# A chunked recurrence's gate: where its constants are finished, who takes an absolute value, and where a logarithm is added

## The chip, the cores and the metric

One core of one Trainium2 chip runs the whole kernel. The metric is the device time in microseconds (us) from the start to the end of one execution. The kernel before took 1930.76 us, the median of 3 runs (1929.14 to 1933.79). TensorE (PE in the profile) multiplies, VectorE (DVE), ScalarE (ACT) and GpSimd (POOL) work on elements, SyncE issues the weight loads.

## The reference

256 tokens of width 1024 pass through one block with gated linear attention and local attention, then through two layers of another kind. Each of these two layers normalizes x, projects it, computes latent attention and a recurrence (`_hgrn2`), and adds the joined result times `w_out` to x; a dense feed-forward part follows in layer 0, eight experts in layer 1. What matters here is the gate of the recurrence:

```python
lb_p = jax.nn.softmax(hg_lower_bounds, axis=0)        # two rows, 512 columns
lower = jnp.cumsum(lb_p, axis=0) - lb_p[0:1]          # layer 0: 0; layer 1: the second row's share
f = lb + (1.0 - lb) * jax.nn.sigmoid(z)
log_f = jnp.log(jnp.maximum(f, F_FLOOR))
k = (1.0 - lb) * jax.nn.sigmoid(-z)
...
b = jnp.cumsum(log_f)                                 # inside a chunk
attn = einsum(q, k, exp(b_t - b_s));  state += (k * exp(b_last - b_s))^T v
```

The lower bound is 0 in layer 0, so there log f and log k need nothing but z. In layer 1 log k = log(1 - lb) + log sigmoid(-z). The kernel computes keys as logarithms: `n_k` holds -log k, and `soft` = ln(1 + exp(-|z|)) serves both log sigmoids.

## The kernel before

All products with large weights run on TensorE in three passes: each weight piece ("sub", 128 x 1024 words) is split into a rounded part `w_hi` (ScalarE, line 1379, in `split_to`) and the rest `w_lo`, which GpSimd makes outside of the feed-forward parts (line 632) and VectorE inside of them. There are four buffers for each, and a piece is 12 matmuls of 512 columns (lines 696 to 698). ScalarE's program interleaves these splits with its own work by hand: `split_to(n)` issues all splits up to piece n, and each of them waits until TensorE has used the piece four before it.

Each engine runs one list of instructions in order, and semaphores join them. TensorE's list for a layer l is: the projections `hf_l` (four pieces, the gate's z), `hq_l` (four), `hg_l` (four), `c0_l`, `c1_l`, `hi_l`, then small products, then the output projection `wo_l` (eight pieces). Between the second and third piece of `hg_l` stands `turn_gate`: the running sums of log f (`hb`, 16 matmuls, line 1026), the turned keys (`hkT`, 8 transposes, line 781) and the tail sums (`ht`, line 1031). Its outputs go to four PSUM banks used in turn, so `ht`, the fifth, waits until VectorE has copied the first `hb` bank out (line 1752). After the fourth piece of `hg_l` the queries are turned (line 781 again), and `level(0)` (line 1049) after the first piece of `c0_l` waits until VectorE has copied them.

The gate on the other engines, in the kernel before:

- VectorE scales z out of PSUM (line 2123), takes |z| (line 2126, recorded at 1768), waits for ScalarE's ln(1 + exp(-|z|)) (lines 1549 and 1551).
- Layer 0: it makes `n_lf` (line 2130) and `n_k` (line 2131), and then finishes the bounds, which only layer 1 reads: a sum (2133), a reciprocal over 512 columns (2134), a product over 1024 (2135, recorded at 1756), and a small constant (2136).
- Layer 1: it forms f in four steps (2140 to 2144), ScalarE takes ln f (1557), VectorE makes `n_lf` (2147) and subtracts log(1 - lb), `log_rest`, from `n_k` over 128 x 1024 (2149).
- Then in both layers the two `hb` banks are copied to `n_bT` (1752), ScalarE makes exp of the turned keys (1562, one instruction of 512 columns a bank), VectorE adds them to `n_bT` (2155, one of 512 a bank), forms the tail keys `n_kt` (2158) and goes on to `level_diff(1)` (two instructions at 2174) and the copies of the turned queries (1752).

Layer 0's output projection `wo_0` takes its input from two splits on VectorE, `split_out("mixT_0", ...)`, the second after the recurrence's output gate. Then VectorE waits for the first half of `wo_0` and adds it to x in `residual` (line 2047). TensorE turns that new x (line 770, `turn_x` in `out_gemm`) before the last piece of `wo_0`.

Of the kernel before, what the change touches and what calls it, by code (L numbers as in the profile page):

```python
# [28 lines left out]
ALU = mybir.AluOpType  # L29
# [157 lines left out]
def build(nc, A, out):  # L187
# [80 lines left out]
    with ExitStack() as ctx:  # L268
        sems = {}

        def sem(name):
            if name not in sems:
                sems[name] = ctx.enter_context(nc.semaphore(name))
            return sems[name]
# [67 lines left out]
        def tiles(ap, t=T):  # L342
            return ap.rearrange("p (t n) -> p t n", t=t)
# [31 lines left out]
        c_gain = [tiny(5) for _ in range(2)]  # L375
        ss, ms, root, rinv, rinv_q = tiny(2 * T), tiny(T), tiny(T), tiny(T), tiny(T)
        least_rest = tiny(1)
        head_ms, head_rinv = tiny(20), tiny(20)
        row_max, sink_exp, row_sum, row_rec = tiny(16), tiny(16), tiny(16), tiny(16)
        sinks = tiny(SWA_HEADS)  # L380
# [922 lines left out]
        def _(act):  # L1303
# [236 lines left out]
            for l in range(2):  # L1540
                squares(range(2 * T), [(f"x_ffn_{l}", q + 1) for q in range(2 * T)], f"ss_l{l}")
                factor(f"l{l}")
                if l == 0:
                    split_to(span["hf_0"][1] + 2)
                    act.wait_ge(sem("bounds_shifted"), 1)
                    act.activation(bounds, bounds, ACT.Exp).then_inc(sem("bounds_exp"), 1)
                split_to(span[f"hf_{l}"][1] + BUFFERS + 1)
                act.wait_ge(sem("z_abs"), l + 1)
                act.activation(n_tmp[0], n_tmp[0], ACT.Exp, scale=-1.0).then_inc(sem("z_odds"), 1)
                act.wait_ge(sem("z_odds"), l + 1)  # L1550
                act.activation(n_tmp[1], n_tmp[0], ACT.Ln, bias=1.0).then_inc(sem("z_soft"), 1)
                if l == 1:
                    act.activation(log_rest, bound_rest, ACT.Ln, bias=least_rest).then_inc(sem("rest_log"), 1)
                split_to(span[f"hg_{l}"][0] + 2)
                if l == 1:
                    act.wait_ge(sem("f_ready"), 1)
# [2 lines left out]
                for t in range(T):  # L1559
                    j = pair_at[f"hkT_{l}"] + t  # L1560
                    act.wait_ge(sem("pair_full"), j + 1)
                    act.activation(n_kT[:, t * 512:(t + 1) * 512], pair_bank[j % 4][:, :], ACT.Exp, scale=-1.0) \
                        .then_inc(sem("k_turned"), 1)
                evacuate(f"hq_{l}", by_token(n_q, 0, func=ACT.Silu))
                evacuate(f"hg_{l}", by_token(n_g, 0, func=ACT.Silu))

# [169 lines left out]
        def _(dve):  # L1736
            told = counter()

            def link(instruction):

                instruction.then_inc(sem("vector_step"), 1)
                dve.wait_ge(sem("vector_step"), told("vector_step"))
# [370 lines left out]
            for l in range(2):  # L2113
# [9 lines left out]
                    dve.tensor_scalar(n_z[:, t, :], gemm_bank[(gemm_at[f"hf_{l}"] + t) % 4][:, :], rinv[:, t:t + 1],  # L2123
                                      LEAST_LOGIT, ALU.mult, ALU.max).then_inc(sem("gemm_read"), 1)
                dve.wait_ge(sem("gemm_read"), gemm_at[f"hf_{l}"] + T)
                absolute(tiles(n_tmp[0]), n_z, "z_abs")
                soft = tiles(n_tmp[1])
                if l == 0:
                    dve.wait_ge(sem("z_soft"), 1)
                    dve.scalar_tensor_tensor(n_lf, n_z, 0.0, soft, ALU.min, ALU.subtract).then_inc(sem("n_lf_ready_0"), 1)  # L2130
                    dve.scalar_tensor_tensor(n_k, n_z, 0.0, soft, ALU.max, ALU.add).then_inc(sem("n_k_ready"), 1)
                    dve.wait_ge(sem("bounds_exp"), 1)
                    link(dve.tensor_tensor(bound_sum, bound_rest, bound_low, ALU.add))
                    link(dve.reciprocal(bound_sum, bound_sum))
                    mul(bounds, bounds, over(bound_sum, 1, 2))
                    link(dve.tensor_scalar(least_rest, ident[:, 0:1], 0.0, LEAST_REST, ALU.mult, ALU.add))
                else:
                    odds, share = tiles(n_tmp[0]), tiles(n_tmp[2])
                    dve.wait_ge(sem("z_odds"), 2)
                    link(dve.scalar_tensor_tensor(share, n_z, 0.0, odds, ALU.is_ge, ALU.max))  # L2140
                    mul(share, share, over(bound_rest, 1, T))
                    dve.wait_ge(sem("z_soft"), 2)
                    link(dve.scalar_tensor_tensor(odds, odds, 1.0, over(bound_low, 1, T), ALU.add, ALU.mult))
                    dve.tensor_tensor(odds, odds, share, ALU.add).then_inc(sem("f_ready"), 1)
                    link(dve.scalar_tensor_tensor(n_k, n_z, 0.0, soft, ALU.max, ALU.add))
                    dve.wait_ge(sem("f_log"), 1)
                    dve.tensor_tensor(n_lf, odds, soft, ALU.subtract).then_inc(sem("n_lf_ready_1"), 1)
                    dve.wait_ge(sem("rest_log"), 1)
                    dve.tensor_tensor(n_k, n_k, over(log_rest, 1, T), ALU.subtract).then_inc(sem("n_k_ready"), 1)
                for t in range(T):  # L2150
                    copy_out(f"hb_{l}", t, n_bT[:, t * 512:(t + 1) * 512])
                for t in range(T):
                    part = slice(t * 512, (t + 1) * 512)
                    dve.wait_ge(sem("k_turned"), T * l + t + 1)
                    dve.tensor_tensor(n_kb[:, part], n_bT[:, part], bank_of(f"hkT_{l}", t)[:, :], ALU.add) \
                        .then_inc(sem("pair_read"), 1)
                    dve.wait_ge(sem("pair_read"), told("pair_read"))
                dve.tensor_tensor(n_kt, bank_of(f"ht_{l}", 0)[:, :], n_k[:, 0, :], ALU.subtract).then_inc(sem("pair_read"), 1)
                dve.wait_ge(sem("pair_read"), told("pair_read"))

                def blocks(a, half):
# [126 lines left out]
                split_out(f"mixT_{l}", banks=range(0, 2), freed=span[f"hi_{l}"][1])  # L2288
                gate_hgrn()
                split_out(f"mixT_{l}", banks=range(2, 4))  # L2290
                residual(f"_{l}", f"x_mixed_{l}", f"g{l}")
                if l == 0:
                    norm("g0")
# [198 lines left out]
```

## Time and profile before

| what | us |
|---|---|
| median of 3 runs | 1930.76 (1929.14 to 1933.79) |
| the profiled execution, whole | 1933.04 |
| its span, first to last instruction | 1931.1 |
| TensorE busy | 1892.8 |
| VectorE busy | 1501.8 |
| ScalarE busy | 1244.5 |
| GpSimd busy | 392.2 |

The span is what the profile covers; 1.9 us of the execution lie around it. Busy time of an engine says how full its list is; what matters for a change is the idle time of TensorE, and what ended each piece of it. Layer 0's gate stands at about 480 to 505 us of the span, its output projection at 588 to 614, layer 1's gate at 813 to 845; the experts begin after 960.

### The profile page before, as it was taken

How to read it: one execution, taken by the hardware profiler on the slowest of the kernel's cores; microseconds unless marked ns; L12 is line 12 of the kernel's file. 1: busy time of each engine (PE TensorE's matmuls, PEld its weight loads, DVE VectorE, ACT ScalarE, POOL GpSimd, SP SyncE). 2: the span in 40 equal slices, each digit the busy share in tenths (PEclk: the TensorE clock that was granted, in tenths of full speed). 3: DMA queues.
4: the chain of work that ended last, by engine and by line, in shares of the span. 5: the costliest groups of instructions: out<-in, count | busy, mean ns of one | idle time of the engine just before them, and what ended most of it. 6: DMA issues, size and time to landing. Idle time of an engine off the chain costs nothing.

```text
span 1931.1 us, 27217 instructions
## 1 busy us (share of the span) xinstructions
PE 1892.8 (98%) x9931; PEld 1610.5 (83%) x9931; DVE 1501.8 (78%) x1598; ACT 1244.5 (64%) x1473; POOL 392.2 (20%) x204
## 2 busy tenths in 40 slices
PE   8999999999999999999899999999999999999997
PEld 6788889998888999878788888888888888888885
DVE  7755366666765756697599999999999999899997
ACT  5654444445644444564388887888888888888885
POOL 5856870002823000372430000000000000000000
PEclk9999999999999999999899999999999999999999
DMA  9434556664443766434399999999999999999994
GB/s 279 154 130 131 175 185 214 216 225 153 140 125 122 226 214 215 156 119 141 131 377 394 382 395 357 395 396 355 395 354 396 396 353 395 355 395 395 358 395 175
DMA packets 251402, 524.54 MB, mean 272 GB/s; under 512 B 10009, under 2 KB 58785, under 8 KB 251185
## 3 DMA queue, kind: packets, MB, share of 16 engines
q1 hardware_dynamic: 244000, 506.36, 73.5%
q10 hardware_dynamic: 5088, 10.03, 1.4%
q0 software_dynamic: 2224, 6.96, 1.1%
q8 instruction: 55, 0.90, 0.2%
q14 instruction: 35, 0.28, 0.0%
HBM read 508.12 MB, written 15.20 MB: 271 GB/s over the span
## 4 chain that ended last, share of the span: by engine, by line
PE 90%; DVE 6%; issue 2%; ACT 2%; POOL 1%; DMA 0%; DVEq 0%; SPq 0%; ACTq 0%
PE bank L696 27%; PE bank L698 27%; PE bank L697 27%; PE bank L1049 2%; PE bank L1222 1%; DVE w_lo_sb L1797 1%; PE bank L770 1%; PE bank L743 1%; PE bank L749 1%; POOL w_lo_sb L632 1%; ACT w_hi_sb L1359 0%; PE bank L1102 0%; PE bank L1100 0%; PE bank L904 0%; PE bank L881 0%
## 5 line engine op out<-in xcount | busy, mean ns | idle before, releaser
L1797 DVE TENSOR_TENSOR w_lo_sb<-arena,w_hi_sb 128x1024 fp32r<-128x1024 f32 x672 | 806.8, 1223 | 73.8 <-ACT w_hi_sb L1359 47.6
L1359 ACT ACTIVATE w_hi_sb<-arena 128x1024 fp32r<-128x1024 f32 x672 | 710.5, 1062 | 165.1 <-PE bank L698 164.6
L696 PE MATMUL bank<-w_hi_sb,left_hi_sb 128*128 128x512 f32 (+1 forms) x1424 | 563.9, 396 | 7.5 <-POOL w_lo_sb L632 3.0
L698 PE MATMUL bank<-w_hi_sb,left_lo_sb 128*128 128x512 f32 (+1 forms) x1424 | 552.7, 388 | 0.0
L697 PE MATMUL bank<-w_lo_sb,left_hi_sb 128*128 128x512 f32 (+1 forms) x1424 | 552.1, 388 | 0.0
L1379 ACT ACTIVATE w_hi_sb<-arena 128x1024 fp32r<-128x1024 f32 (+1 forms) x269 | 280.3, 1052 | 336.6 <-PE bank L698 325.2
L632 POOL TENSOR_TENSOR w_lo_sb<-arena,w_hi_sb 128x1024 fp32r<-128x1024 f32 (+1 forms) x134 | 343.0, 2580 | 566.2 <-ACT w_hi_sb L1379 565.7
L696 PEld LDWEIGHTS bank<-w_hi_sb,left_hi_sb 128*128 128x128 f32 x1424 | 268.4, 188 | 66.4 <-issue 6.3
L698 PEld LDWEIGHTS bank<-w_hi_sb,left_lo_sb 128*128 128x128 f32 x1424 | 268.2, 188 | 56.1
L697 PEld LDWEIGHTS bank<-w_lo_sb,left_hi_sb 128*128 128x128 f32 x1424 | 268.5, 189 | 52.2 <-issue 0.7
L1809 DVE TENSOR_TENSOR w_lo_sb<-arena,w_hi_sb 128x1024 fp32r<-128x1024 f32 x135 | 163.8, 1219 | 126.1 <-ACT w_hi_sb L1379 125.1
L696 PE MATMUL bank<-w_hi_sb,hid_hi_sb 128*128 128x512 f32 x656 | 257.3, 392 | 0.0
L697 PE MATMUL bank<-w_lo_sb,hid_hi_sb 128*128 128x512 f32 x656 | 255.5, 389 | 0.0
L698 PE MATMUL bank<-w_hi_sb,hid_lo_sb 128*128 128x512 f32 x656 | 255.4, 389 | 0.0
L696 PE MATMUL bank<-left_hi_sb,w_hi_sb 128*128 128x256 f32 (+1 forms) x712 | 201.7, 283 | 0.1
L698 PE MATMUL bank<-left_hi_sb,w_lo_sb 128*128 128x256 f32 (+1 forms) x712 | 201.4, 283 | 0.0
L697 PE MATMUL bank<-left_lo_sb,w_hi_sb 128*128 128x256 f32 (+1 forms) x712 | 201.4, 283 | 0.0
L687 POOL DMA_INDIRECT h_sb<-returned,arena x2 | 2.6, 1278 | 841.9 <-DMA returned<-arena 841.6
L698 PEld LDWEIGHTS bank<-w_hi_sb,hid_lo_sb 128*128 128x128 f32 x656 | 123.1, 188 | 26.0
L696 PEld LDWEIGHTS bank<-w_hi_sb,hid_hi_sb 128*128 128x128 f32 x656 | 123.3, 188 | 24.4
L697 PEld LDWEIGHTS bank<-w_lo_sb,hid_hi_sb 128*128 128x128 f32 x656 | 123.4, 188 | 24.2
L696 PEld LDWEIGHTS bank<-left_hi_sb,w_hi_sb 128*128 128x128 f32 (+1 forms) x712 | 135.9, 191 | 1.2 <-DVE w_lo_sb L1809 0.3
(328 smaller groups left out, 1628.3 us busy)
## 6 DMA issues: line engine op xcount, KB each, us to landing
arena<-in_moe_w_gate SPq DMA_DIRECT2D x112, 1024.0 KB, 7.8
arena<-in_moe_w_up SPq DMA_DIRECT2D x112, 1024.0 KB, 7.8
arena<-in_moe_w_down SPq DMA_DIRECT2D x112, 1024.0 KB, 7.6
arena<-in_w_in SPq DMA_DIRECT2D x45, 1024.0 KB, 5.1
arena<-in_w_ffn_in SPq DMA_DIRECT2D x22, 1024.0 KB, 6.2
arena<-in_w_out SPq DMA_DIRECT2D x12, 1024.0 KB, 5.0
arena<-in_w_ffn_out SPq DMA_DIRECT2D x11, 1024.0 KB, 4.8
arena<-in_dense_w_gate SPq DMA_DIRECT2D x11, 1024.0 KB, 5.9
```

Of the source, the lines that this page charges most:

```text
L632: pool.tensor_tensor(buffer(w_lo_sb, j, k, n), w, buffer(w_hi_sb, j, k, n).bitcast(F32), ALU.subtract).then_inc(sem("w_lo_by_gpsimd"), 1)
L696: pe.matmul(out, still[0], moving[0], start=start, stop=False)
L697: pe.matmul(out, still[0], moving[1], start=False, stop=False)
L698: return pe.matmul(out, still[1], moving[0], start=False, stop=stop)
L743: pe.matmul(gemm_bank[turned % 4][:, j * TOKENS:(j + 1) * TOKENS], w[:, k, j, 0:NOPE], n_cT[:, first + k, :], start=(k == 0), stop=(k == k ...
L749: mm = pe.matmul(o, n_cT[:, first + k, t * P:(t + 1) * P], w[:, k, :, NOPE:], start=(k == 0), stop=(k == k_tiles - 1))
L770: tr = pe.transpose(b[:, at:at + P], source(k, t), ident)
L1049: mm = pe.matmul(b[:, i * P:(i + 1) * P], key[:, at:at + P], query[:, at:at + P], start=True, stop=True)
L1359: act.activation(expert_buffer(w_hi_sb, j), expert_piece(j % MOE_SUBS), ACT.Copy) \
L1379: act.activation(buffer(w_hi_sb, j, *w.shape[1:]), w, ACT.Copy).then_inc(sem("w_hi_ready"), 1)
L1797: dve.tensor_tensor(expert_buffer(w_lo_sb, j), expert_piece(j % MOE_SUBS), expert_buffer(w_hi_sb, j).bitcast(F32), ALU.subtract) \
L1809: dve.tensor_tensor(buffer(w_lo_sb, j, *w.shape[1:]), w, buffer(w_hi_sb, j, *w.shape[1:]).bitcast(F32), ALU.subtract) \
```

## The change

- In layer 0 the bounds are no longer finished after `n_k`, but after the second `mixT_0` split and ahead of `residual`. Two instructions join them there: the product of `bound_rest` with the identity (128 x 512) and its sum over the last axis, which turns 1 - lb so that it lies along partitions, one column for each of the four heads (`rest_turned`).
- |z| is taken by ScalarE with `Abs` in both layers, ahead of the exponential. The one split that stood ahead of the exponential now stands behind it.
- In layer 1 `n_k` is no longer reduced by `log_rest`. ScalarE takes one more small logarithm (`rest_turned`, 128 x 4), and its exp of the turned keys becomes four instructions of 128 columns a bank with a bias column each. VectorE's add to `n_bT` becomes four `scalar_tensor_tensor` of 128 columns a bank, and `n_kt` gets `log_rest` in a second instruction (128 x 512).

```diff
-                split_to(span[f"hf_{l}"][1] + BUFFERS + 1)
+                split_to(span[f"hf_{l}"][1] + BUFFERS)
+                act.wait_ge(sem("gemm_read"), gemm_at[f"hf_{l}"] + T)
+                act.activation(tiles(n_tmp[0]), n_z, ACT.Abs).then_inc(sem("z_abs"), 1)
                 act.wait_ge(sem("z_abs"), l + 1)
                 act.activation(n_tmp[0], n_tmp[0], ACT.Exp, scale=-1.0).then_inc(sem("z_odds"), 1)
                 act.wait_ge(sem("z_odds"), l + 1)
+                split_to(span[f"hf_{l}"][1] + BUFFERS + 1)
                 act.activation(n_tmp[1], n_tmp[0], ACT.Ln, bias=1.0).then_inc(sem("z_soft"), 1)
                 if l == 1:
                     act.activation(log_rest, bound_rest, ACT.Ln, bias=least_rest).then_inc(sem("rest_log"), 1)
+                    act.activation(rest_turned, rest_turned, ACT.Ln, bias=least_rest).then_inc(sem("rest_log"), 1)
...
-                    act.activation(n_kT[:, t * 512:(t + 1) * 512], pair_bank[j % 4][:, :], ACT.Exp, scale=-1.0) \
-                        .then_inc(sem("k_turned"), 1)
+                    # layer 0 as before; layer 1:
+                    for i in range(HG_HEADS):
+                        ins = act.activation(n_kT[:, t * 512 + i * P:t * 512 + (i + 1) * P],
+                                             pair_bank[j % 4][:, i * P:(i + 1) * P], ACT.Exp,
+                                             bias=rest_turned[:, i:i + 1], scale=-1.0)
+                    ins.then_inc(sem("k_turned"), 1)
...
-                absolute(tiles(n_tmp[0]), n_z, "z_abs")
...
-                    dve.wait_ge(sem("bounds_exp"), 1)
-                    link(dve.tensor_tensor(bound_sum, bound_rest, bound_low, ALU.add))
-                    link(dve.reciprocal(bound_sum, bound_sum))
-                    mul(bounds, bounds, over(bound_sum, 1, 2))
-                    link(dve.tensor_scalar(least_rest, ident[:, 0:1], 0.0, LEAST_REST, ALU.mult, ALU.add))
...
-                    dve.wait_ge(sem("rest_log"), 1)
-                    dve.tensor_tensor(n_k, n_k, over(log_rest, 1, T), ALU.subtract).then_inc(sem("n_k_ready"), 1)
...
+                        dve.wait_ge(sem("rest_log"), 2)
+                        for i in range(HG_HEADS):
+                            at = slice(t * 512 + i * P, t * 512 + (i + 1) * P)
+                            ins = dve.scalar_tensor_tensor(n_kb[:, at], turned[:, i * P:(i + 1) * P],
+                                                           rest_turned[:, i:i + 1], n_bT[:, at], ALU.subtract, ALU.add)
...
+                    link(dve.tensor_tensor(n_kt, bank_of(f"ht_{l}", 0)[:, :], n_k[:, 0, :], ALU.subtract))
+                    dve.tensor_tensor(n_kt, n_kt, log_rest, ALU.add).then_inc(sem("pair_read"), 1)
...
                 split_out(f"mixT_{l}", banks=range(2, 4))
+                if l == 0:
+                    dve.wait_ge(sem("bounds_exp"), 1)
+                    link(dve.tensor_tensor(bound_sum, bound_rest, bound_low, ALU.add))
+                    link(dve.reciprocal(bound_sum, bound_sum))
+                    mul(bounds, bounds, over(bound_sum, 1, 2))
+                    link(dve.tensor_scalar(least_rest, ident[:, 0:1], 0.0, LEAST_REST, ALU.mult, ALU.add))
+                    picked = n_tmp[2][:, 0:512].rearrange("p (g d) -> p g d", d=P)
+                    mul(picked, bound_rest.rearrange("p (g d) -> p g d", d=P), over(ident, 1, HG_HEADS))
+                    link(dve.tensor_reduce(rest_turned, picked, AX_X, ALU.add))
                 residual(f"_{l}", f"x_mixed_{l}", f"g{l}")
```

## Rows read from the trace of the kernel before

**Rows 1.** The page, engines: busy us, share of the span, instructions.
```profile
PE 1892.8 (98%) x9931; PEld 1610.5 (83%) x9931; DVE 1501.8 (78%) x1598; ACT 1244.5 (64%) x1473; POOL 392.2 (20%) x204
```
**Rows 2.** TensorE's waits, 476 to 620 us: total us, times, longest.
```profile
PE bank L1031 <- DVE arena L1752: 1.4, 1, 1.4
PE bank L696 <- POOL w_lo_sb L632: 0.7, 2, 0.4
```
**Rows 3.** TensorE's waits, 800 to 935 us.
```profile
PE bank L1026 <- DVE arena L2147: 1.8, 1, 1.8
PE bank L781 <- DVE arena L2149: 1.3, 1, 1.3
PE bank L696 <- POOL w_lo_sb L632: 0.3, 1, 0.3
```
**Rows 4.** VectorE in order of time, layer 0's gate: start us, us, what.
```profile
481.36 2.32 DVE L1768 SCALAR_TENSOR_TENSOR arena<-arena 128x1024 f32<-128x1024 f32 x1
...
489.32 3.42 DVE L2131 SCALAR_TENSOR_TENSOR arena<-arena 128x1024 f32<-128x1024 f32 x1
492.67 2.88 DVE L2133 TENSOR_TENSOR arena<-const_sb 128x512 f32<-128x512 f32 x1
495.58 3.35 DVE L2134 RECIPROCAL arena<-arena 128x512 f32<-128x512 f32 x1
498.96 2.25 DVE L1756 TENSOR_TENSOR const_sb<-const_sb,arena 128x1024 f32<-128x1024 f32 x1
```
**Rows 5.** GpSimd in order of time, layer 0's gate.
```profile
482.55 3.40 POOL L632 TENSOR_TENSOR w_lo_sb<-arena,w_hi_sb 128x1024 fp32r<-128x1024 f32 x1
```
**Rows 6.** ScalarE in order of time, layer 0's gate (idle before, its releaser).
```profile
483.41 1.06 ACT L1379 ACTIVATE w_hi_sb<-arena 128x1024 fp32r<-128x1024 f32 x1 [1.09 <-PE bank L698]
```
**Rows 7.** VectorE in order of time, layer 0's output projection.
```profile
605.56 1.28 DVE L2047 TENSOR_TENSOR x_sb<-x_sb,bank 128x512 f32<-128x512 f32 x2 [5.76 <-PE bank L698]
```
**Rows 8.** GpSimd in order of time, the same stretch.
```profile
597.63 2.40 POOL L632 TENSOR_TENSOR w_lo_sb<-arena,w_hi_sb 128x1024 fp32r<-128x1024 f32 x1 [0.39 <-ACT w_hi_sb L1379]
...
603.97 2.40 POOL L632 TENSOR_TENSOR w_lo_sb<-arena,w_hi_sb 128x1024 fp32r<-128x1024 f32 x1 [0.38 <-ACT w_hi_sb L1379]
606.63 2.39 POOL L632 TENSOR_TENSOR w_lo_sb<-arena,w_hi_sb 128x1024 fp32r<-128x1024 f32 x1 [0.26 <-ACT w_hi_sb L1379]
```
**Rows 9.** TensorE in order of time, turning the new x.
```profile
608.02 1.03 PE L770 MATMUL bank<-const_sb,x_sb 128*128 128x128 f32 x8
```
**Rows 10.** VectorE in order of time, layer 1's gate.
```profile
828.53 1.23 DVE L2144 TENSOR_TENSOR arena<-arena 128x1024 f32<-128x1024 f32 x1
...
839.09 4.35 DVE L2174 TENSOR_TENSOR arena<-arena 128x512 f32<-128x512 f32 x2
843.45 1.42 DVE L1752 COPY arena<-bank 128x512 f32<-128x512 f32 x2
```
**Rows 11.** ScalarE in order of time, layer 1's gate.
```profile
829.79 1.06 ACT L1557 ACTIVATE arena<-arena 128x1024 f32<-128x1024 f32 x1 [6.16 <-DVE arena L2144]
830.76 3.88 ACT L1379 ACTIVATE w_hi_sb<-arena 128x1024 fp32r<-128x1024 f32 x4
834.65 1.28 ACT L1562 ACT_TABLE_LOAD   x1
```
**Rows 12.** TensorE in order of time, layer 1.
```profile
835.54 1.09 PE L781 MATMUL bank<-const_sb,arena 128*128 128x128 f32 x8 [1.26 <-DVE arena L2149]
...
846.41 1.95 PE L1049 MATMUL bank<-arena 128*128 128x128 f32 x16
```
**Rows 13.** Groups by line and shape: count, busy us, mean ns.
```profile
L1786 DVE SCALAR_TENSOR_TENSOR left_lo_sb<-bank,small_sb,left_hi_sb 128x256 fp32r<-128x256 f32 x48 | 21.0, 480 | 0.8
L1455 ACT ACTIVATE h_sb<-h_sb,small_sb 128x128 f32<-128x128 f32 x8 | 3.1, 390 | 4.9 <-DVE small_sb L1764 4.9
```
**Rows 14.** Busy time in two stretches: PE, PEld, DVE, ACT, POOL, granted clock, DMA share, GB/s.
```profile
813.00:846.00 33.00, 29.67 (x143) 23.82 (x143) 30.59 (x20) 22.18 (x24) 28.54 (x11) 1.00 0.43 135
...
952.00:962.50 10.50, 7.37 (x36) 6.63 (x34) 6.75 (x26) 4.01 (x8) 2.72 (x4) 0.51 0.17 52
```

More of the change, by code:

```diff
@@ L377, in build @@
         least_rest = tiny(1)
+        rest_turned = tiny(HG_HEADS)
         head_ms, head_rinv = tiny(20), tiny(20)
@@ L1561, in _ @@
                     act.wait_ge(sem("pair_full"), j + 1)
-                    act.activation(n_kT[:, t * 512:(t + 1) * 512], pair_bank[j % 4][:, :], ACT.Exp, scale=-1.0) \
-                        .then_inc(sem("k_turned"), 1)
+                    if l == 0:
+                        act.activation(n_kT[:, t * 512:(t + 1) * 512], pair_bank[j % 4][:, :], ACT.Exp, scale=-1.0) \
+                            .then_inc(sem("k_turned"), 1)
+                        continue
+                    if t == 0:
+                        act.wait_ge(sem("rest_log"), 2)
+                    for i in range(HG_HEADS):
[3 more added lines that the diff above has]
+                    ins.then_inc(sem("k_turned"), 1)
                 evacuate(f"hq_{l}", by_token(n_q, 0, func=ACT.Silu))
@@ L2144, in _ @@
                     dve.tensor_tensor(odds, odds, share, ALU.add).then_inc(sem("f_ready"), 1)
-                    link(dve.scalar_tensor_tensor(n_k, n_z, 0.0, soft, ALU.max, ALU.add))
+                    dve.scalar_tensor_tensor(n_k, n_z, 0.0, soft, ALU.max, ALU.add).then_inc(sem("n_k_ready"), 1)
                     dve.wait_ge(sem("f_log"), 1)
                     dve.tensor_tensor(n_lf, odds, soft, ALU.subtract).then_inc(sem("n_lf_ready_1"), 1)
-                    dve.wait_ge(sem("rest_log"), 1)
-                    dve.tensor_tensor(n_k, n_k, over(log_rest, 1, T), ALU.subtract).then_inc(sem("n_k_ready"), 1)
                 for t in range(T):
@@ L2154, in _ @@
                     dve.wait_ge(sem("k_turned"), T * l + t + 1)
-                    dve.tensor_tensor(n_kb[:, part], n_bT[:, part], bank_of(f"hkT_{l}", t)[:, :], ALU.add) \
+                    turned = bank_of(f"hkT_{l}", t)
+                    if l == 0:
+                        dve.tensor_tensor(n_kb[:, part], n_bT[:, part], turned[:, :], ALU.add) \
+                            .then_inc(sem("pair_read"), 1)
+                    else:
+                        dve.wait_ge(sem("rest_log"), 2)
[3 more added lines that the diff above has]
+                                                           rest_turned[:, i:i + 1], n_bT[:, at], ALU.subtract, ALU.add)
+                        ins.then_inc(sem("pair_read"), 1)
+                    dve.wait_ge(sem("pair_read"), told("pair_read"))
+                if l == 0:
+                    dve.tensor_tensor(n_kt, bank_of(f"ht_{l}", 0)[:, :], n_k[:, 0, :], ALU.subtract) \
                         .then_inc(sem("pair_read"), 1)
-                    dve.wait_ge(sem("pair_read"), told("pair_read"))
-                dve.tensor_tensor(n_kt, bank_of(f"ht_{l}", 0)[:, :], n_k[:, 0, :], ALU.subtract).then_inc(sem("pair_read"), 1)
+                else:
+                    link(dve.tensor_tensor(n_kt, bank_of(f"ht_{l}", 0)[:, :], n_k[:, 0, :], ALU.subtract))
+                    dve.tensor_tensor(n_kt, n_kt, log_rest, ALU.add).then_inc(sem("pair_read"), 1)
                 dve.wait_ge(sem("pair_read"), told("pair_read"))
@@ L2290, in _ @@
                 split_out(f"mixT_{l}", banks=range(2, 4))
+                if l == 0:
+                    dve.wait_ge(sem("bounds_exp"), 1)
[6 more added lines that the diff above has]
+                    link(dve.tensor_reduce(rest_turned, picked, AX_X, ALU.add))
                 residual(f"_{l}", f"x_mixed_{l}", f"g{l}")
```

## The prediction

> **What bounds the kernel now.** I read the page first, then TensorE's waits around the two gates, then the instructions in order of time on each engine there. On the page TensorE is busy for 1892.8 of 1931.1 us [rows 1]: the kernel ends with TensorE, and an edit elsewhere is worth only the TensorE idle time that it ends or makes. The waits name that idle time. Layer 0's gate has 1.4 us before the tail sums (the first `hb` bank was not copied out, because VectorE was still finishing the bounds) and 0.7 us in two waits for GpSimd's `w_lo` [rows 2]. Layer 1's gate has 1.8 us for `n_lf`, 1.3 us for `n_k` and 0.3 us for GpSimd [rows 3].
>
> The order of time shows a second thing, on which most of this prediction rests. A `w_lo` piece takes GpSimd 2.40 us [rows 8], but 3.40 us while VectorE works on two SBUF operands [rows 5]. Four VectorE instructions of the gate are long as well: the 512-wide sum takes 2.88 us and the 1024-wide ones 2.25 to 3.42 us [rows 4], where a free 1024-wide one takes 1.23 us [rows 10] and a 512-wide one reading PSUM takes about 0.7 us (two in 1.42 us, [rows 10]). The two engines take turns: each such VectorE instruction lets a running GpSimd piece finish, and the next piece waits for it. Instructions on PSUM keep their length beside GpSimd. The Trainium skill (SBUF — State Buffer, section "Who interferes with whom") says the same as a rule: a VectorE instruction with two SBUF inputs and a GpSimd one that reads SBUF exclude each other for their whole length, and whichever issues first wins; the trace agrees (2.88 us against about 0.7).
>
> **Layer 0's gate: minus 2.5 us.** The bounds leave: 8.5 us of VectorE from 492.67 on, so that the `hb` bank is copied as soon as it is full, and the 1.4 us wait goes. |z| leaves VectorE (2.32 us, [rows 4]); it stood between two GpSimd pieces and cost the second 1.0 us (3.40 against 2.40, [rows 5, 8]). With |z|, the sum and the product gone, GpSimd's pieces come 1 to 2 us sooner, which ends one wait of 0.3 us of the two in [rows 2] (the other, 0.4 us, stands at 480.29, ahead of the change) and some slow restarts, by my estimate another 0.5 to 0.8 us. What ScalarE gains, `Abs`, is hidden: its 1.06 us (taken from the 1024-wide logarithm, [rows 11]) fall into the 1.09 us in which ScalarE waited for TensorE to free a buffer [rows 6], and that split now runs behind the exponential; the logarithm starts at the same time. `n_lf` may lose 1.4 us to a GpSimd piece, still 5 us ahead of its reader. Without the GpSimd part the gain is 1.4 us; with every stall gone it is 2.8 us. I take 2.5.
>
> No row shows an `Abs`. If it made ScalarE load its table again, that would cost 1.28 us as at [rows 11], once in each layer, between nothing and 1.3 us on `n_lf`, of which layer 0 hides all and layer 1 part. The Trainium skill (ScalarE: Activation LUTs, "Table sets: the hidden batching unit") says that `abs` lies in every set, hence no load; the sum is the same by it.
>
> **Layer 0's output projection: plus 3.4 us.** VectorE is free from 599.80, and `residual` starts at 605.56 after 5.76 us of idle time [rows 7]. TensorE wants the new x at 608.02 [rows 9]; `residual`'s two adds end at 606.84, so it may come 1.2 us late at no cost. Into this gap go: sum 0.7 + reciprocal 3.35 [rows 4] + product 1.2 + constant 0.15 + product with the identity 0.7 + reduction 0.7 + five links of 0.03, together 6.95 us. With no other engine in the way they end at 606.75, `residual` at 608.05: a cost of about 0.1 us, the lower bound. But both products have two SBUF operands, and GpSimd works through this stretch [rows 8]. The sum waits until the piece of 597.63 ends at 600.0 [rows 8] and ends at 600.6; the reciprocal (one operand; 3.35 us beside GpSimd already) ends at 603.98; the big product issues at about 604.02, GpSimd's piece at 603.97.
> - If GpSimd wins: product from 606.4 to 607.5, next piece (issued at 606.63) to 609.9, product with the identity to 610.5, reduction to 611.2. `residual` starts 5.7 us late; minus 1.2 of slack, TensorE waits 4.5 us.
> - If VectorE wins: product to 605.2, piece to 607.6, identity product to 608.2, reduction to 608.9: 3.4 late, TensorE waits 2.2 us.
>
> The order hangs on 0.05 us, which I can't call; I take the middle, 3.4, and keep 0.1 and 4.5 as bounds. Everything behind `residual` (the split of the turned x, the squares, ScalarE's splits) moves with it; GpSimd is a piece or two ahead of TensorE there and absorbs its own delay.
>
> **Layer 1's gate: plus 1.1 us.** First the gain. |z| on ScalarE saves up to 1.3 us before the exponential, but the f chain then falls between GpSimd's pieces again: followed piece by piece, f is ready at about 829.1 instead of 829.76 [rows 10]. So `n_lf` ends 0.7 us sooner and the first `hb` matmul starts at 831.55 instead of 832.24. `n_k` is ready before it, its subtraction gone: the 1.3 us wait before the transposes goes [rows 3]. TensorE leaves `turn_gate` 2.1 to 2.2 us sooner and would be at `level(0)` at 844.3 instead of 846.41 [rows 12].
>
> But `level(0)` needs the turned queries, which VectorE copies behind `level_diff(1)`; before, those copies end at 844.87 [rows 10], 1.5 us ahead. Their new time: ScalarE runs ln f and the four splits 0.7 us sooner, loads its table and starts the exponentials at 835.25 [rows 11]. They are now eight of 390 ns [rows 13]; back to back I take 0.3 us each, 2.4 us together (1.09 before), so they end at 837.7. VectorE's eight 128-wide adds, read down from 480 ns at 256 columns [rows 13], take 1.2 us a bank and follow ScalarE: 838.9 instead of 838.33. The tail keys take 0.7 us, to 839.6; their second instruction has two SBUF operands and waits for GpSimd, which has a backlog of four pieces from 831.5 on (to 840.95): it ends at 841.55. So `level_diff(1)` starts 2.4 us later than 839.09. Its two instructions take turns with GpSimd:
> - If GpSimd's next piece (issued at about 841.3) is ahead of the first, they end at 847.5, the copies at 848.95: `level(0)` at 849.0, plus 2.6 us.
> - If it comes after, they end at 845.1, the copies at 846.5: plus 0.1 us.
> - If the second tail instruction finds GpSimd free: copies at 845.9, minus 0.4 us.
> - Were VectorE not the later one at all, the whole 2.2 us would stay.
>
> I take plus 1.1, between the first two. Later readers in the layer have 2.7 us or more to spare.
>
> **Sum.** -2.5 + 3.4 + 1.1 = +2.0 us. The profiled execution took 1933.04, 2.3 above the median of the runs; against the median the forecast is 1932.8 us.
>
> **The rivals.**
> - *The moved work is covered and both gates keep their gain.* Layer 0 gains 2.5 and loses 0.1, layer 1 gains 0.4 to 2.2: 2.8 to 4.6 us faster, about 1927. For it: VectorE did idle 5.76 us where the bounds go. Against it: that idle time is shorter than the work even without GpSimd, and GpSimd is busy for more than two thirds of it. Chance 0.22.
> - *VectorE becomes the bound in both places, each time because a GpSimd piece gets in ahead.* Place: before `turn_x` in `wo_0` and before `level(0)` in layer 1. Price: 4.5 + 2.6 - 2.5 = +4.6 us, 1935.4. It decides by whether the products issue after 603.97 and the first difference after about 841.3. Chance 0.20.
> - *The longer wait drops TensorE's clock.* After the router's waits the granted clock is 0.51 for 10.5 us [rows 14], that is 1.2 GHz, with TensorE busy 7.37 us. A 4.5 us wait at 608 might do the same and cost up to 5 us more: 1938 to 1940. Against it, TensorE was idle for 3.3 of 33 us around layer 1's gate and the clock stayed at 1.00, that is 2.4 GHz [rows 14]. Chance 0.05.
> - *The forecast*, gains and new waits that nearly cancel, 1930.3 to 1934.5: 0.53.
>
> A measurement of this kernel tells a change from none at about 0.2%, 3.9 us. Of the first rival three fifths lie beyond it (0.14 faster, and 0.02 for what I overlooked); of the second most and the third all (0.22). The rest, 0.62, is within. The range 1927.0 to 1936.5 reaches to both sides.
>
> **What would show each step.** Right: no wait of line 1031 for 1752 in layer 0; GpSimd's pieces near 2.4 us from 482 on; no wait for `n_k` in layer 1; a new wait of TensorE at `turn_x` (line 770 family) for `residual` of 2 to 4.5 us, with the two products of the bounds longer than 1.2 and 0.7 us; a new wait at `level(0)` for the query copies. The prediction is wrong if the product with the identity takes 0.7 us and `turn_x` doesn't wait, or if `level_diff(1)` starts before 840.

## The result: 0.5% slower, outside the predicted range

| | before | after |
|---|---|---|
| median, us | 1929.26 (1929.11 to 1933.79, 5 runs) | 1939.96 (1938.98 to 1940.96, 5 runs) |
| ratio | 1 | 1.0050, 95% interval 1.0039 to 1.0061 |
| profiled execution, us | 1933.04 | 1938.98 |
| its span, us | 1931.1 | 1937.1 |
| granted clock, mean | 0.996 | 0.991 |

The forecast was 1932.8 us, in a range of 1927.0 to 1936.5. The change costs about 10 us, and 2.0 were expected. First the page of the kernel after, engines as in [rows 1], and the granted clock in 40 slices:

```profile
PE 1895.5 (98%) x9931; PEld 1613.5 (83%) x9931; DVE 1489.4 (77%) x1604; ACT 1247.9 (64%) x1482; POOL 385.7 (20%) x204
...
PEclk9999999999998999999899999999999999999999
```

VectorE works 12.4 us less, and TensorE has as many instructions as before but is busy 2.7 us longer. So something other than waiting has been added: the same matmuls took longer. Next TensorE's waits from 476 to 620 us, which answer to [rows 2] (us in total, times, longest):

```profile
PE bank L771 <- DVE x_sb L2061: 4.1, 1, 4.1
...
PE bank L697 <- POOL w_lo_sb L633: 0.4, 1, 0.4
```

and from 800 to 935 us, which answer to [rows 3]:

```profile
PE bank L1050 <- DVE arena L1766: 3.8, 1, 3.8
...
PE bank L1027 <- DVE arena L2155: 1.4, 1, 1.4
```

The waits for `hb` in layer 0 and for `n_k` in layer 1 are gone, and two new ones stand at `turn_x` (L771, 770 before) and `level(0)` (L1050, 1049 before). Here is where TensorE stood at its landmarks. The two profiled executions already differ by 3.36 us far ahead of the change: TensorE comes to the kernel's first turned keys (L782, 781 before) at 76.93 us instead of 80.29. About 2.0 us of this come from the first large products, which ran at half speed in the profile before; the rest is a longer wait for GpSimd there. TensorE, before and then after:

```profile
11.15 0.63 PE L697 MATMUL bank<-w_lo_sb,left_hi_sb 128*128 128x512 f32 x1
```
```profile
10.98 0.40 PE L698 MATMUL bank<-w_lo_sb,left_hi_sb 128*128 128x512 f32 x1
```

This start comes and goes by itself: of the 12 profiles of this document three reach that place at 80.3 to 80.6 us (before, e3 and e13) and nine at 76.4 to 78.1. In the column "later by" the 3.36 us are therefore added to the times of after before the difference is taken.

| TensorE begins | before | after | later by | step since the row above |
|---|---|---|---|---|
| L0 `hb` | 497.94 | 493.43 | -1.15 | gate |
| L0 tail sums | 502.19 | 496.08 | -2.75 | -1.6, gate |
| L0 second `mixT` half | 596.23 | 591.66 | -1.21 | +1.5, no new wait |
| L0 `turn_x` | 608.02 | 607.73 | +3.07 | +4.3, the new wait |
| L1 last `turn_x` | 804.16 | 806.43 | +5.63 | +2.6, no new wait |
| L1 turned queries | 842.81 | 842.57 | +3.12 | -2.5, gate |
| L1 `level(0)` | 846.41 | 850.18 | +7.13 | +4.0, the new wait |
| L1 `level(1)` | 856.38 | 862.70 | +9.68 | +2.6, no new wait |

Three steps come without a wait. The granted clock explains them. Busy time in four stretches of the kernel after (columns as in [rows 14]):

```profile
582.50:586.00 3.50, 3.50 (x10) 2.68 (x10) 3.33 (x6) 0.00 (x0) 0.00 (x0) 0.54 0.00 0
606.50:613.30 6.80, 5.57 (x18) 4.75 (x19) 4.31 (x8) 2.37 (x6) 2.37 (x1) 0.52 0.38 145
849.00:855.70 6.70, 5.52 (x22) 5.13 (x23) 4.64 (x8) 3.78 (x6) 1.82 (x1) 0.53 0.31 90
958.00:968.30 10.30, 7.17 (x34) 6.18 (x35) 6.82 (x28) 4.39 (x7) 2.09 (x2) 0.52 0.16 53
```

and in the same places of the kernel before (3.4 us apart from them at most):

```profile
585.00:590.00 5.00, 3.15 (x18) 2.35 (x16) 4.27 (x8) 0.66 (x3) 0.00 (x0) 1.00 0.00 0
606.00:614.00 8.00, 8.00 (x50) 7.12 (x49) 5.27 (x10) 5.11 (x12) 6.20 (x4) 1.00 0.65 234
846.00:853.00 7.00, 7.00 (x41) 6.09 (x40) 6.86 (x7) 5.81 (x9) 4.17 (x2) 1.00 0.49 162
```

The last stretch of the four is the router's, which the kernel before has too [rows 14]. The other three are new: TensorE ran at 1.2 GHz for 3.4, 6.8 and 6.8 us, from 582.3, 606.2 and 848.5 on. The second began 2.6 us into the idle time before `turn_x`, the third 2.2 us into the idle time before `level(0)`; both went on behind the end of the wait. So:

- waits and gains: -2.8 + 4.3 - 2.5 + 4.0 = +3.0 us;
- clock: 1.5 + 2.6 + 2.6 = +6.7 us.

The sum is 9.7 us, against 10.7 between the two medians. It is not a matter of one profile: the mean granted clock was 0.990 to 0.993 in all five executions of the kernel after, and 0.994 to 0.997 in the 28 of the kernel before that were measured beside e5 to e10.

How the two waits arise stands in VectorE's list. Layer 0's output projection, VectorE (start us, us):

```profile
595.27 0.74 DVE L2313 TENSOR_TENSOR arena<-const_sb 128x512 f32<-128x512 f32 x1
596.04 3.35 DVE L2314 RECIPROCAL arena<-arena 128x512 f32<-128x512 f32 x1
599.43 3.44 DVE L1770 TENSOR_TENSOR const_sb<-const_sb,arena 128x1024 f32<-128x1024 f32 x1
...
603.09 2.54 DVE L1770 TENSOR_TENSOR arena<-const_sb 128x512 f32<-128x512 f32 x1
605.67 0.69 DVE L2319 TENSOR_REDUCE small_sb<-arena 128x4 f32<-128x512 f32 x1
606.39 1.28 DVE L2061 TENSOR_TENSOR x_sb<-x_sb,bank 128x512 f32<-128x512 f32 x2
```

and GpSimd beside it:

```profile
599.39 2.40 POOL L633 TENSOR_TENSOR w_lo_sb<-arena,w_hi_sb 128x1024 fp32r<-128x1024 f32 x1 [0.38 <-ACT w_hi_sb L1380]
602.05 3.04 POOL L633 TENSOR_TENSOR w_lo_sb<-arena,w_hi_sb 128x1024 fp32r<-128x1024 f32 x1 [0.26 <-ACT w_hi_sb L1380]
```

GpSimd's piece starts 0.04 us ahead of the big product. The product takes 3.44 us where a free one takes 1.2, so it waited 2.2 us for that piece; the next piece waits for the product (3.04 instead of 2.40), and the product with the identity waits for that piece (2.54 instead of about 0.7). Layer 1, VectorE:

```profile
838.49 2.29 DVE L2169 SCALAR_TENSOR_TENSOR arena<-bank,small_sb,arena 128x128 f32<-128x128 f32 x8 [2.18 <-ACT arena L1574]
840.81 0.69 DVE L2177 TENSOR_TENSOR arena<-bank,arena 128x512 f32<-128x512 f32 x1
841.53 1.71 DVE L2178 TENSOR_TENSOR arena<-arena 128x512 f32<-128x512 f32 x1
843.27 5.53 DVE L2194 TENSOR_TENSOR arena<-arena 128x512 f32<-128x512 f32 x2
848.73 1.40 DVE L1766 COPY arena<-bank 128x512 f32<-128x512 f32 x2
```

with GpSimd (0.24 us ahead of the first difference) and ScalarE:

```profile
843.03 5.23 POOL L633 TENSOR_TENSOR w_lo_sb<-arena,w_hi_sb 128x1024 fp32r<-128x1024 f32 x2 [0.33 <-ACT w_hi_sb L1380]
```
```profile
835.95 1.28 ACT L1574 ACT_TABLE_LOAD   x1
837.24 2.18 ACT L1574 ACTIVATE arena<-bank,small_sb 128x128 f32<-128x128 f32 x8
```

The two differences take 5.53 us for work of 1.4, and the copies that `level(0)` wants stand behind them.

### The profile page after: what moved, and what is told of

The parts are those of the page before. It is cut to its first block, busy times and chain, and to the rows that moved or that the text cites. A ratio compares the mean times of both kernels' runs of the same rounds, so it can differ in the third digit from the quotient of the medians.

```text
span 1937.1 us, 27234 instructions
## 1 busy us (share of the span) xinstructions
PE 1895.5 (98%) x9931; PEld 1613.5 (83%) x9931; DVE 1489.4 (77%) x1604; ACT 1247.9 (64%) x1482; POOL 385.7 (20%) x204
## 4 chain that ended last, share of the span: by engine, by line
PE 89%; DVE 6%; issue 2%; ACT 1%; DMA 1%; POOL 1%; DVEq 0%; SPq 0%; ACTq 0%; POOLq 0%
PE bank L697 26%; PE bank L699 26%; PE bank L698 26%; PE bank L1050 2%; PE bank L1223 1%; DVE w_lo_sb L1811 1%; PE bank L771 1%; PE bank L744 1%; POOL w_lo_sb L633 1%; PE bank L750 1%; DMA const_sb<-in_const_table 1%; DMA arena<-in_w_in 0%; ACT w_hi_sb L1360 0%; PE bank L1103 0%; PE bank L1101 0%
## 5 line engine op out<-in xcount | busy, mean ns | idle before, releaser
L633 POOL TENSOR_TENSOR w_lo_sb<-arena,w_hi_sb 128x1024 fp32r<-128x1024 f32 (+1 forms) x134 | 336.9, 2532 | 578.6 <-ACT w_hi_sb L1380 578.3
L699 PEld LDWEIGHTS bank<-w_hi_sb,hid_lo_sb 128*128 128x128 f32 x656 | 123.1, 188 | 25.9
```

Source lines behind the costliest of these rows:

```text
L633: pool.tensor_tensor(buffer(w_lo_sb, j, k, n), w, buffer(w_hi_sb, j, k, n).bitcast(F32), ALU.subtract).then_inc(sem("w_lo_by_gpsimd"), 1)
L699: return pe.matmul(out, still[1], moving[0], start=False, stop=stop)
```

## The experiments

Ratios are to the kernel before on the same chip in the same session, with a 95% interval; the medians of before were 1931.15 us for e1 to e4, 1930.26 for e5 to e10 and 1930.02 for e12 and e13; that of after was measured against 1929.26, so between kernels of different sessions the ratios say more than the medians. The theory at the outset: two waits, each from VectorE and GpSimd taking turns, and each followed by a stretch at 1.2 GHz that costs more than the forecast had put on it. The rival: the clock is low in this kernel for a reason of its own, and the waits alone don't carry the loss.

### e1_bounds_only: before, with only the four bounds instructions moved ahead of residual

```diff
 # layer 0's gate
-                    link(dve.tensor_tensor(bound_sum, bound_rest, bound_low, ALU.add))
-                    ... reciprocal, product, constant
 # behind split_out("mixT_0", banks 2 to 3)
+                    the same four
```

> The kernel before with one edit: layer 0's bounds (sum, reciprocal, product, constant) are finished ahead of residual; nothing is turned. Theory (VectorE's lateness makes a TensorE wait, and a wait of about 4 us is followed by a stretch at 1.2 GHz): layer 0's gate gains 1.4 to 2.2 us; without the identity product and the reduction the residual comes 3.2 us sooner than in the changed kernel, so TensorE waits 0.7 to 1 us for it, too short for the clock to fall: 0.5 to 1.5 us faster than before. Rival (any new wait at that place costs the 1.2 GHz stretch): 1 to 2 us slower than before. Rival (the move itself gives back nothing): 2 us faster.

Measured: 1930.0 us (1928.44 to 1930.98, 11 runs), ratio 0.9993 (0.9984 to 1.0002). TensorE's wait at `turn_x`, and VectorE's big product, of this kernel:

```profile
PE bank L770 <- DVE x_sb L2047: 0.8, 1, 0.8
```
```profile
598.49 3.45 DVE L1756 TENSOR_TENSOR const_sb<-const_sb,arena 128x1024 f32<-128x1024 f32 x1
```

The big product waits for GpSimd just as in the kernel after, and still TensorE waits only 0.8 us, with no low clock behind it. So moving the bounds is harmless by itself. What turns 0.8 us into 4.1 are the product with the identity and its reduction (3.3 us with their links). A gain isn't shown either: the interval includes 1. By the landmarks of its profile layer 0's gate gains 1.6 us, `turn_x` takes 1.0 back, and a stretch of 3.4 us at 1.2 GHz at 918, in front of `wo_1`, takes 1.6.

### e2_abs_only: before, with only |z| on ScalarE

```diff
-                absolute(tiles(n_tmp[0]), n_z, "z_abs")
+                act.activation(tiles(n_tmp[0]), n_z, ACT.Abs).then_inc(sem("z_abs"), 1)
```

(The split ahead of the exponential moves behind it, as in the kernel after.)

> The kernel before with one edit: the absolute value by ScalarE in both layers. Theory: GpSimd's pieces in layer 0's gate come sooner, about 0.5 us there, and in layer 1 n_lf is ready 0.5 to 1 us sooner: 0.5 to 1.5 us faster, no new wait, clock as before. Rival (Abs costs a table load or delays the exponential): 0 to 2 us slower.

Measured: 1934.03 us (1931.54 to 1935.34, 11 runs), ratio 1.0014 (1.0005 to 1.0023): slower, where a gain was expected, and for another reason than the rival's: no table load stands between `Abs` and the exponential. TensorE's wait in layer 0's gate, and a window right behind it:

```profile
PE bank L1031 <- DVE arena L1755: 3.9, 1, 3.9
```
```profile
502.00:506.00 4.00, 4.00 (x12) 3.12 (x11) 2.59 (x4) 0.00 (x0) 0.00 (x0) 0.58 0.76 245
```

TensorE gets to `turn_gate` 1.2 us sooner, but the bounds still stand ahead of the `hb` copy. They end 1.3 us later than before, counted from the same start, because `n_lf` ahead of them now waits for a GpSimd piece (2.82 us instead of 1.50, VectorE). The wait of 1.4 us [rows 2] becomes 3.9, and a stretch of 3.4 us at 1.2 GHz starts at 501.9 and goes on into the window above. It costs 1.65 us, and the layer ends up 2.9 us late. Freeing an engine ahead of a fixed obstacle made the gap longer and took the clock with it.

### e3_turned_only: after, with the bounds and the turning back in the gate and |z| on VectorE

```diff
 # layer 0's gate, behind n_k
+                    the four bounds instructions
+                    mul(picked, bound_rest..., over(ident, 1, HG_HEADS))
+                    link(dve.tensor_reduce(rest_turned, picked, AX_X, ALU.add))
```

> The changed kernel with the bounds and the two turning instructions back in layer 0's gate and the absolute value back on VectorE: only the keys' log of the rest is handled the new way. Theory: layer 0's gate loses up to 3 us (two more VectorE instructions ahead of the first hb copy), layer 1's gate gains 1.3 us (no wait for n_k), and then the query copies are late: a wait of 2 to 4 us before level(0) and, behind it, about 7 us at 1.2 GHz that cost 2.5 us: 5 to 8 us slower than before. Rival (layer 1's loss came from the combination with the earlier gate, not from the split exponentials and adds): within 3 us of before.

Measured: 1940.19 us (1938.47 to 1942.18, 5 runs), ratio 1.0043 (1.0029 to 1.0057). Waits in layer 0 and in layer 1:

```profile
PE bank L1032 <- DVE arena L1763: 4.7, 1, 4.7
```
```profile
PE bank L1050 <- DVE arena L1763: 3.8, 1, 3.8
```

The loss is as large as in the kernel after with the turning in a quite different place: low stretches go with both waits (6.8 us from 503.3, 3.4 us from 854.9). Nearly the whole loss belongs to the turned keys: the two instructions that prepare them, in either place, and the longer chain in front of the query copies.

### e4_spread: after, with the bounds and the turning finished between units of the feed-forward part

```diff
-                if l == 0: (ahead of residual) the six instructions
+                    if tag == "f2" and 3 <= u < 7:
+                        finish_bounds(u - 3)      # sum | reciprocal | product | turning
```

> The changed kernel with the bounds and the turning finished one instruction or two per unit in the feed-forward part f2, where GpSimd is idle, instead of ahead of residual. Theory: the 4.1 us wait for the residual and the 1.2 GHz stretch behind it (2.6 us) go, all else stays: 6 to 7 us faster than the changed kernel, 1933 to 1934. Rival (the clock falls there for another reason): only the wait goes, about 1936.

Measured: 1931.83 us (1929.03 to 1935.08, 11 runs), ratio 1.0002 (0.9993 to 1.0011). In that part GpSimd makes no pieces. TensorE's waits in layer 0's gate and output projection hold nothing of the bounds any more:

```profile
PE bank L1148 <- DVE h_sb L1770: 0.4, 1, 0.4
PE bank L697 <- POOL w_lo_sb L633: 0.4, 1, 0.4
```

Between the medians 8.1 us come back, by the ratios 9.3 (0.48% of 1930). The first wait and the stretch at 1.2 GHz behind it account for 6.9 (4.3 + 2.6); the stretch at 582, absent in this profile, is another 1.5, and the stretch behind `level(0)` is 3.4 us long instead of 6.8 and costs 0.8 less. Layer 1's wait of 3.8 us is still there.

### e5_warm: after, with overwritten matmuls in both waits

```diff
+                for _ in range(count):   # 16 ahead of turn_x, 15 ahead of level(0)
+                    pe.matmul(bank[:, :], left_hi_sb[:, 0:P], left_hi_sb[:, 0:512], start=True, stop=True)
```

> The changed kernel with matmuls on data at hand, whose results are overwritten, put into TensorE's two new waits: 16 of 512 columns (3.6 us) ahead of the wait for the residual, 15 (3.4 us) ahead of level(0) in layer 1. Nothing else moves. Theory (TensorE's idleness in the waits makes the clock fall behind them): the waits stay as long, but the stretches at 1.2 GHz behind them are gone: 4 to 5 us faster than the changed kernel, 1935 to 1936. Rival (the clock falls for what runs behind the waits, or by chance): no change, 1940.

Measured: 1934.54 us (1932.57 to 1938.02, 8 runs), ratio 1.0024 (1.0013 to 1.0034). This one separates wait from clock: VectorE and GpSimd do what they do in the kernel after, TensorE is as late at both places (+4.3 and +4.1 us as in the table above), but not idle. The two stretches:

```profile
604.00:614.00 10.00, 9.45 (x63) 8.32 (x63) 6.99 (x13) 4.66 (x11) 4.81 (x2) 1.00 0.33 107
846.00:856.00 10.00, 9.81 (x51) 8.46 (x52) 9.14 (x10) 4.73 (x7) 5.15 (x3) 1.00 0.23 74
```

The clock stays at 1.00 and 5.4 us come back (5.0 by the ratios), though useless work was added. Over its eight executions the mean granted clock is 0.9952, against 0.9956 of before. Of the loss of 0.50% the clock behind the two waits is half (0.26 points of it). The other half is 4.6 us by the ratio (2.5 to 6.6), and the waits less the gains, 3.0 us, lie within that. So the rival fails for these two stretches: the clock falls because TensorE is idle.

### e6_reorder: e4_spread, with layer 1's query copies ahead of the differences

```diff
+                if l == 0:
                     level_diff(1)
                 for t in range(T):
                     copy_out(f"hqT_{l}", t, n_qT[:, t * 512:(t + 1) * 512])
+                if l == 1:
+                    level_diff(1)
```

(In layer 1 `level_diff(2)` also stands later.)

> e4_spread with layer 1's list on VectorE in another order: the turned queries are copied ahead of level_diff(1), and level_diff(2) comes behind level_scale(1) and the n_qd product. Theory (level(0) waits only because the copies stand behind level_diff(1), which takes turns with GpSimd): the 3.8 us wait at level(0) goes, up to 2 us come back as waits at level(1) to level(3) because VectorE is late as a whole by about 4 us: 2 to 5 us faster than e4_spread, 1927 to 1930. Rival (VectorE's total work in this stretch is the limit, the order doesn't matter): the wait moves to a later level whole, 1931 to 1932.

Measured: 1927.91 us (1924.38 to 1932.19, 11 runs), ratio 0.9989 (0.9980 to 0.9998). VectorE in layer 1:

```profile
834.86 1.42 DVE L1766 COPY arena<-bank 128x512 f32<-128x512 f32 x2
836.31 4.11 DVE L2211 TENSOR_TENSOR arena<-arena 128x512 f32<-128x512 f32 x2
```

The copies read PSUM, wait for nobody and take their 1.42 us; the wait of TensorE at `level(0)` is gone, and with it the low clock. The differences still take turns with GpSimd (4.11 us), and all that this leaves is a wait of 0.8 us for a later step. With both losses repaired the whole change gains 2 us. The profiled execution is the fastest of the eleven (1924.38 us, granted clock 0.996); the slowest took 1932.19 us at 0.992, so low stretches still come in some executions, and where they lie there isn't known.

### e8_memset: after, with GpSimd's pieces near the bounds set to zero

```diff
+                    if span["wo0_0"][0] <= j < span["wo1_0"][1]:
+                        pool.memset(buffer(w_lo_sb, j, k, n).bitcast(F32), 0.0)...
+                        continue
```

These pieces' low parts are left out of the products, so that GpSimd only writes.

> The changed kernel, except that GpSimd fills the w_lo pieces of layer 0's output projection with zeros instead of subtracting (so that product lacks its low part): GpSimd then reads nothing there. Theory (VectorE's instructions with two SBUF operands and GpSimd's reading ones exclude each other): the bounds' product takes 1.2 us instead of 3.4 and the identity product 0.7 instead of 2.5, the residual starts about 4 us sooner, TensorE's wait falls from 4.1 us to under 0.5 and the 1.2 GHz stretch behind it goes: 5 to 7 us faster than the changed kernel. Rival (those products are slow for their shapes or for writing const_sb): durations and time stay.

Measured: 1935.26 us (1932.62 to 1937.07, 8 runs), ratio 1.0025 (1.0014 to 1.0035). The range of pieces was chosen too short: the two beside the bounds' products were still subtractions. VectorE, then GpSimd:

```profile
599.15 1.22 DVE L1773 TENSOR_TENSOR const_sb<-const_sb,arena 128x1024 f32<-128x1024 f32 x1
600.41 0.15 DVE L2319 TENSOR_SCALAR small_sb<-const_sb 128x1 f32<-128x1 f32 x1
600.60 2.58 DVE L1773 TENSOR_TENSOR arena<-const_sb 128x512 f32<-128x512 f32 x1
```
```profile
596.36 0.96 POOL L634 MEMSET w_lo_sb<- 128x1024 f32 x1 [2.60 <-ACT w_hi_sb L1383]
599.16 6.24 POOL L636 TENSOR_TENSOR w_lo_sb<-arena,w_hi_sb 128x1024 fp32r<-128x1024 f32 x2 [1.84 <-ACT w_hi_sb L1383]
```

The miss shows more than the plan would have. Here VectorE issued the big product 0.01 us ahead of GpSimd's piece and it took 1.22 us; in the kernel after it issued 0.04 us behind and took 3.44. This is the prediction's other branch: TensorE waits 1.9 us where 2.2 was worked out. (The Trainium skill, SBUF — State Buffer, section "Who interferes with whom", says that the order of issue decides which of the two is held up; these two rows, with 0.05 us between them, agree.) The low stretch behind that shorter wait is 3.4 us instead of 6.8. So this run tests the order of issue; what a GpSimd that reads nothing does beside these two products was not run.

### e10_gate0_only: before, with |z| on ScalarE and the bounds in the feed-forward part, keys as before

```diff
 # e2_abs_only, and of e4_spread the steps sum | reciprocal | product
```

> The kernel before with the absolute value by ScalarE and the bounds finished inside the feed-forward part f2 (three units, one or two instructions each); layer 1's keys as before. Theory: layer 0's gate gains 2.8 us and layer 1's 0.9 us (as in e2_abs_only), no new wait: 3 to 4 us faster than before, 1927 to 1928. Rival (gaining in the gate shifts what comes after so that the clock falls elsewhere, as in e1_bounds_only behind 918 us): 1 to 2 us faster.

Measured: 1927.93 us (1926.21 to 1929.75, 11 runs), ratio 0.9988 (0.9979 to 0.9997). Without any turned key this is as fast as e6_reorder. Layer 0's gate keeps its 2.9 us, and layer 1 still has its waits for `n_lf` and `n_k`:

```profile
PE bank L1026 <- DVE arena L2157: 1.5, 1, 1.5
...
PE bank L781 <- DVE arena L2159: 1.3, 1, 1.3
```

So |z| on ScalarE, the culprit of e2_abs_only, does no harm once nothing stands ahead of the copy. In the profiles it is a gain: the gate comes 2.8 us sooner here and 1.6 in e1_bounds_only, and layer 1's another 1.0. The ratios of the two runs overlap, so they don't show it.

### e12_warm_router: e6_reorder, with nine overwritten matmuls in the router's wait for the mask

```diff
             b = pair("ranks", 0)
+            keep_warm(b, 9)
             pe.wait_ge(sem("e_mask_ready"), 1)
```

> The version with the bounds in the feed-forward part and the query copies ahead of the differences, plus nine overwritten matmuls of 512 columns in TensorE's 2.3 us wait for the experts' mask. Theory (the low stretch at the router comes from its waits): the stretch of 6.8 us at 1.2 GHz there shrinks to 3.4 us or goes, and the time falls by 1.6 to 3.3 us against the version without them, to about 0.9975 of before. Rival (the low clock there comes from the sparse 128-column matmuls and the 1.4 and 0.8 us waits ahead of the mask): the stretch stays, and the time stays within 0.5 us of 0.999 of before.

Measured: 1926.45 us (1923.58 to 1930.44, 11 runs), ratio 0.9984 (0.9975 to 0.9993), the lowest ratio of all. The wait of 2.3 us is filled, and of the router's 6.8 us at 1.2 GHz in e6_reorder 3.4 are left (950.1 to 953.5):

```profile
950.40:953.80 3.40, 3.40 (x19) 3.40 (x19) 2.65 (x4) 0.34 (x1) 2.72 (x4) 0.54 0.02 5
```

The expected gain of 1.6 us or more is not shown: 0.5 thousandths, 1 us, lie between two ratios whose intervals overlap. What is left of the stretch has TensorE busy throughout, behind sparse work with waits of 1.4 and 0.8 us. The 3.4 us are the shortest of the 12 profiles, but the router's stretch varies without any filler: 10.2 us in seven of them, 6.8 in three, 13.7 in one.

### e13_warm_turn_x: after, with the fillers only ahead of turn_x

```diff
+                    if name == "hT_g0" and i == 0:
+                        keep_warm(pair(name, first + i), 16)
```

> The kernel after with sixteen overwritten matmuls of 512 columns only in the wait of turn_x, none in the wait of level(0). Theory (each wait sets its own low stretch): no low stretch at 606, that at 849 stays, time some 2.6 us under the kernel after, about 1.0037 of before. The stretch of 3.4 us at 582 lies ahead of the filled wait, so by the theory it stays as often as in the kernel after; if it goes too, it was not caused by what follows it but comes and goes by itself. Rival (the low stretches are one chain, the first setting the later ones, or a budget that is spent anyway): the one at 849 goes too, or the one at 606 only moves, and the time is 5 us or 0 us under the kernel after.

Measured: 1936.36 us (1934.06 to 1939.28, 8 runs), ratio 1.0031 (1.0021 to 1.0042). Two windows, behind `turn_x` and behind `level(0)`:

```profile
607.00:614.00 7.00, 6.45 (x36) 5.26 (x35) 5.94 (x11) 2.89 (x7) 2.40 (x1) 1.00 0.40 150
849.50:854.00 4.50, 4.41 (x21) 4.24 (x22) 2.69 (x5) 2.71 (x5) 1.40 (x1) 0.62 0.33 122
```

The stretch behind the filled wait is gone and the one behind the other stays, so each wait sets its own; they are no chain. The time is 3.6 us under the kernel after, where 2.6 were expected. The second is 3.4 us long here (1.7 us of loss) where it was 6.8 in the kernel after, behind the same wait of 3.8 us. The stretch at 582 is absent too, although the kernel up to there is that of after.

## Why the prediction was wrong

- *Layer 0's gate, minus 2.5.* Right: -2.8. The wait for `hb` went and one wait for GpSimd went. GpSimd's ten pieces from 477 us on took 25.9 us instead of 29.0: eight took 2.4 us each, and the two beside `n_lf` and `n_k` 3.4. `Abs` (L1550) loaded no table, the exponential (L1552) starts 1.1 us behind it:

```profile
478.86 1.04 ACT L1550 ACTIVATE arena<-arena 128x1024 f32<-128x1024 f32 x1
479.94 1.06 ACT L1552 ACTIVATE arena<-arena 128x1024 f32<-128x1024 f32 x1
```

  (The Trainium skill, ScalarE: Activation LUTs, section "Table sets: the hidden batching unit", says that `abs` is in every set; these two rows agree.)
- *Layer 0's output projection, plus 3.4.* The mechanism was right in each of its links, and the branch in which GpSimd wins came true: 4.3 us where 4.5 was worked out. To take the middle of two branches that hang on hundredths of a microsecond was a choice of no case that exists.
- *Layer 1's gate, plus 1.1.* Right: -2.5 gained (2.1 to 2.2 expected), 4.0 lost, net +1.5. The eight exponentials took 2.18 us (2.4 expected), the eight adds 2.29 (2.4), the second tail instruction 1.71 (1.95), and GpSimd came ahead of the first difference. For that branch the prediction had +2.6. Measured from where TensorE enters the layer, the differences began 0.5 us sooner than it had worked out, and they took 5.5 us for 5.95. The +1.1 of the sum is again a middle of two branches, and that it comes near +1.5 is luck.
- *The sum without the clock*: +3.0 measured, +2.0 forecast; 0.9 of the difference is the middle taken at `turn_x`. That alone would have given about 1934, inside the range.
- *The clock: the step that failed.* The sum -2.5 + 3.4 + 1.1 has no term for TensorE's clock; it was put at nothing, and measured it is +6.7 us, of which +5.2 are behind the two waits. The third rival said that a longer wait drops TensorE's clock, "A 4.5 us wait at 608 might do the same and cost up to 5 us more", and got a chance of 0.05. It happened at 606.2 and again at 848.5, and e5_warm and e13_warm_turn_x show that the idle time is the cause. That its 1938 to 1940 us was met is partly luck: it reckoned with one place at up to 5 us, and there were two at 2.6 and one at 1.5. The argument against it rested on the clock staying at 1.00 where TensorE was idle for 3.3 of 33 us [rows 14]. But that idle time came in parts of 1.8, 1.3 and 0.3 us [rows 3], and the forecast itself held a new wait of 2.2 to 4.5 us. A total over 33 us said nothing of one unbroken wait; the largest single one that [rows 2] and [rows 3] show with a full clock is 1.8 us. A branch with a wait above that lay outside what the rows showed and needed a price of its own. The profile before has a bound for it: 10.5 us at half speed with 7.37 busy [rows 14] lose up to 3.7 us; 2.6 were measured behind each wait.
- *The rivals.* "Covered" failed at its own point, the length of the gap. "VectorE becomes the bound in both places" came true at both places (4.3 for 4.5; in layer 1 +1.5 for +2.6), and came with the clock on top. The two were treated as exclusive cases, when the clock follows from the wait.

Open: 1.5 us of the profiled execution come from the stretch of 3.4 us at 582.3, in front of `wo_0`. Ahead of it stand small products with gaps of 0.3, 0.4 and 1.4 us in every version. It shows in 2 of the 12 profiles (after, e8_memset), and the same stage of layer 1 has one in 4 (e1, e2, e10, e13). No run settles what decides it, so it can't be laid to the change. Nor is it known whether the other four executions of after had it: only their mean clock is on record.

## What to carry to other kernels

Price a new TensorE wait twice, as the wait and as what the clock does behind it: here waits of 0.8 and 1.8 us cost only themselves, those of 3.8 to 4.7 us cost 1.6 to 2.6 us more, and the 1.9 us one was followed by a low stretch too. Compare two profiles by the steps between landmarks, since these two differ by 3.4 us ahead of the change. Before an engine gets slack work into a gap, look at which engine it takes turns with there; the same six instructions cost 4.3 us of waiting beside GpSimd's subtractions and nothing in the feed-forward part. And what a critical transfer waits behind can often be moved: two copies put ahead of two differences gave back all of layer 1's loss.

## What the runs showed of the hardware

- The low stretches up to the router's were 3.4, 6.8 or 10.2 us long in the 12 profiles, and 13.7 once (the router in e10_gate0_only). The same wait of 3.8 us at `level(0)` was followed by 6.8 us in the kernel after and in e8_memset, but by 3.4 us in e4_spread and e13_warm_turn_x. So the same wait has two prices.
- 512-column matmuls that were thrown away held the clock at 1.00 through waits of about 4 us, and the program with more work was 5.4 us faster.
- A difference of 0.05 us in the order of issue moved a 1024-wide product between 1.22 and 3.44 us.
